# A two-block network on one core: GpSimd makes all four token combinations of the feed-forward layers, in pieces of 512 columns

## The reference, cut to what matters

```python
def swiglu(h, w_in, w_out):
    gu = h @ w_in
    gate, up = jnp.split(gu, 2, axis=-1)
    return (jax.nn.silu(gate) * up) @ w_out
...
for i in range(DEPTH):                # DEPTH = 2
    ...                               # attention, x = x + g1 * y
    h = rmsnorm(x, norm_ffn[i]) * (1 + sc2) + sh2
    x = x + g2 * swiglu(h, ffn_w_in[i], ffn_w_out[i])
```

## Time and profile before

| | us |
|---|---|
| median of 3 runs | 2672.32 |
| lowest, highest | 2672.22, 2672.35 |
| the profiled execution, its own time | 2670.46 |
| span of the profiled execution, first to last instruction | 2668.7 |

### The profile page before, as it was taken

How to read it: one execution, slowest core, us unless ns; L and a number is a source line. 1 busy time by engine, 2 the same in 40 slices (tenths; PEclk the granted TensorE clock), 3 DMA queues, 4 the chain that set the end, 5 groups by cost and what they waited for, 6 DMA issues and landing times. The chain is left out here.

```text
span 2668.7 us, 35605 instructions
## 1 busy us (share of the span) xinstructions
PE 2588.7 (97%) x12898; PEld 2063.0 (77%) x12898; DVE 1885.1 (71%) x3089; ACT 1022.1 (38%) x1833; POOL 331.5 (12%) x455
## 2 busy tenths in 40 slices
PE   6999899999999999999999989999999999999998
PEld 5666587788888888777776768888888887888987
DVE  6888857877777777745656788777777777433565
ACT  5444726333333333445445453333333333111243
POOL 2011003000000000201110210000000027971000
PEclk9999999999999999999999999999999999999999
DMA  6333221111111111223232111111111122113122
GB/s 238 116 129 135 92 90 52 56 51 55 54 52 48 55 55 44 105 68 97 94 105 88 48 32 56 51 51 55 51 55 47 55 63 92 48 48 58 32 95 79
DMA packets 170955, 193.10 MB, mean 72 GB/s; under 512 B 8000, under 2 KB 136224, under 8 KB 170432
## 3 DMA queue, kind: packets, MB, share of 16 engines
q1 hardware_dynamic: 158256, 147.45, 17.1%
q0 software_dynamic: 12592, 44.21, 5.4%
HBM read 177.86 MB, written 12.58 MB: 71 GB/s over the span
## 5 line engine op out<-in xcount | busy, mean ns | idle before, releaser
L2534 DVE SCALAR_TENSOR_TENSOR xT<-psum,mod,xT 128x1024 f32<-128x1024 f32 x352 | 446.2, 1279 | 146.1 <-PE psum L1506 146.0
L1506 PE MATMUL psum<-hT_high,w_low 128*128 128x512 f32 x1344 | 360.5, 390 | 6.7 <-DVE xT L2534 6.6
L1506 PEld LDWEIGHTS psum<-hT_high,w_low 128*128 128x128 f32 x1344 | 251.6, 188 | 62.7 <-DVE xT L2534 11.0
L1964 ACT ACTIVATE w_high<-wpair 128x512 fp32r<-128x512 f32 x294 | 184.8, 632 | 244.3 <-DMA wpair<-in_ffn_w_in_dram 132.8
L1192 PE MATMUL psum<-hT_high,w_low 128*128 128x512 f32 x864 | 244.2, 395 | 2.3 <-DVE arena L3047 2.1
L1506 PE MATMUL psum<-h_low,w_low 128*128 128x512 f32 x672 | 207.6, 390 | 2.2 <-DVE h_low L2529 2.2
L1275 PE MATMUL psum<-hT_high,w_low 128*128 128x512 f32 x480 | 202.1, 421 | 0.9 <-DVE h_low_mix L2472 0.7
L1474 PE MATMUL psum<-hT_high,w_high 128*128 128x512 f32 x504 | 196.6, 390 | 0.0
L1475 PE MATMUL psum<-h_low,w_high 128*128 128x512 f32 x504 | 196.6, 390 | 0.0
L1476 PE MATMUL psum<-hT_high,w_low 128*128 128x512 f32 x504 | 196.4, 390 | 0.0
L1192 PEld LDWEIGHTS psum<-hT_high,w_low 128*128 128x128 f32 x864 | 162.6, 190 | 39.1 <-issue 2.5
(11 more groups left out here) (380 smaller groups left out, 5156.0 us busy)
## 6 DMA issues: line engine op xcount, KB each, us to landing
wpair<-in_ffn_w_in_dram SPq DMA_DIRECT2D x176, 256.0 KB, 2.9
wpair<-in_ffn_w_out_dram SPq DMA_DIRECT2D x88, 256.0 KB, 2.7
wpair<-in_ada_tiles_dram POOLq DMA_DIRECT2D x20, 1024.0 KB, 5.3
wpair<-in_ada_tiles_dram POOLq DMA_DIRECT2D x32, 512.0 KB, 3.6
wpair<-in_w_in_dram SPq DMA_DIRECT2D x24, 512.0 KB, 3.8
wpair<-in_b_tiles_dram SPq DMA_DIRECT2D x18, 512.0 KB, 3.3
arena<-in_ada_tiles_dram SPq DMA_DIRECT2D x8, 1024.0 KB, 16.3
out_dram<-xT SPq DMA_DIRECT2D x16, 512.0 KB, 3.3
```

The lines of the kernel that those rows point to most:

```text
L1506: mm = nc.tensor.matmul(dst[:, HALF * t:HALF * t + HALF], w, src[:, t, :], start=n == 0, stop=n == 2)
L1964: nc.scalar.activation(part_high[name], part_raw[name], ACT.Copy).then_inc(part_high_ready, 1)
L2534: nc.vector.scalar_tensor_tensor(xT[:, m, :], acc[m % 2] if src is None else src, mod[:, l, 40 + m:41 + m], xT[:, m, :], ALU.mult, ALU.add ...
```

## The change

GpSimd makes all four combinations, each in four pieces of 512 columns (16 instructions a layer where there were 6), in the order T1, T3, T2, T4. A piece waits for the pieces that it reads, for the `shift` of the chunk that it reads, and, before it overwrites a raw chunk, for the `half_low` that still reads it. T3 and T4 leave VectorE's list (two instructions of 128 x 2048 a layer). T3's high part takes the place of T1's on ScalarE, and the other way round; T3's low part moves ahead of the first two `add_down` on VectorE. The low parts of T2 and T1 get a second wait, for the combination that still reads the raw values.

```diff
+TOKEN_TURN = ("T1", "T3", "T2", "T4")
+HIGH_TOKENS = ("T3", "T1", "T2", "T4")
...
+def token_number(f, name):
+
+    return 16 * f + 4 * TOKEN_TURN.index(name) + 4
...
                     pool.wait_ge(shifted, shift_number(2 * f + 1, k))
                     nc.gpsimd.tensor_tensor(h_low[:, k, 0:HALF], token_raw[quadrant[0][k // 4]][:, k % 4, :], as_f32(hT_high[:, k, 0:HALF]),
                                             ALU.subtract).then_inc(front_ready, 1)
-                for k in range(4):
-                    pool.wait_ge(shifted, shift_number(2 * f + 1, k, 1))
-                    nc.gpsimd.tensor_tensor(token_raw["T1"][:, k, :], token_raw["T3"][:, k, :], token_raw["B11"][:, k, :],
-                                            ALU.subtract).then_inc(token_made, 1)
-                for n in range(2):
-                    rows = slice(2 * n, 2 * n + 2)
-                    pool.wait_ge(token_made, 8 * f + n + 5)
-                    nc.gpsimd.tensor_tensor(token_raw["T2"][:, rows, :], token_raw["T2"][:, rows, :], token_raw["T1"][:, rows, :],
-                                            ALU.subtract).then_inc(token_made, 1)
+                for n, (name, x, y, read, shift) in enumerate((("T1", "T3", "B11", None, 0), ("T3", "T2", "T3", 0, 4),
+                                                               ("T2", "T2", "T1", 4, None), ("T4", "T4", "T2", None, None))):
+                    for k in range(4):
+                        if n:
+                            pool.wait_ge(token_made, 16 * f + 4 * n + k - 3)
+                        if shift is not None:
+                            pool.wait_ge(shifted, shift_number(2 * f + 1, shift + k, 1))
+                        if read is not None:
+                            pool.wait_ge(h_ready, h_number(2 * f + 1, read + k))
+                        nc.gpsimd.tensor_tensor(token_raw[name][:, k, :], token_raw[x][:, k, :], token_raw[y][:, k, :],
+                                                ALU.subtract).then_inc(token_made, 1)
...
-                def token(n, name):
-
-                    act.wait_ge(token_made, 8 * f + n + 4)
+                def token(name):
+
+                    act.wait_ge(token_made, token_number(f, name))
                     nc.scalar.activation(token_high[name], token_raw[name], ACT.Copy).then_inc(token_high_ready, 1)
...
-                    token(1, "T3")
+                    token("T1")
                     keep(1, "P3", gate_half[:, 1, :], bank["c"])
                     high(1, "S1")
-                    token(3, "T2")
+                    token("T2")
...
-                    token(4, "T4")
+                    token("T4")
...
                 hidden_high(0, 0, first=True)
-                token(0, "T1")
+                token("T3")
                 second_step()
...
-                def token(n, name, x, y, ks):
-
-                    dve.wait_ge(token_made, 8 * f + n + 4)
-                    nc.vector.tensor_tensor(token_raw[name][:, ks], token_raw[x][:, ks], token_raw[y][:, ks], ALU.subtract).then_inc(token_made, 1)
-
-                def token_lows(n, name):
-
-                    dve.wait_ge(token_high_ready, 4 * f + n + 1)
+                def token_lows(name, after):
+
+                    dve.wait_ge(token_high_ready, 4 * f + HIGH_TOKENS.index(name) + 1)
+                    if after:
+                        dve.wait_ge(token_made, token_number(f, after))
                     nc.vector.tensor_tensor(token_low[name], token_raw[name], as_f32(token_high[name]), ALU.subtract).then_inc(token_split, 1)
...
-                    token(0, "T3", "T2", "T3", slice(0, 4))
+                    token_lows("T3", None)
                     add_down(0, 0)
                     add_down(0, 1)
-                    token_lows(1, "T3")
                     add_down(0, 2)
                     down_lows(0, 1)
                     low(1, "S2")
                     combine(1, "S1", first=True)
-                    token(3, "T4", "T4", "T2", slice(0, 4))
-                    token_lows(2, "T2")
+                    token_lows("T2", "T4")
                     dve.wait_ge(product_kept, kept_number(f, 1, "P1"))
                     add(1, "X0", gate_half[:, 0, :], gate_half[:, 0, :], bank["b"], "P2")
                     low(1, "S1")
-                    token_lows(0, "T1")
+                    token_lows("T1", "T2")
                     add_down(0, 3)
                     low(1, "A22")
-                    token_lows(3, "T4")
+                    token_lows("T4", None)
```

## The result

The changed kernel takes 2682.62 us (median of five runs, 2679.87 to 2683.89) against 2672.22 (five runs): ratio 1.0041 [1.0028, 1.0055], slower by 0.4%. The profiled execution took 2681.51 us, span 2679.7; before 2670.46 and 2668.7.

A forecast was written before the change was run, and what follows sets the result against it. PE, 97% busy, was taken as the bound, with VectorE's list setting the pace before the loop. Two layers at +5.3 us give 10.6 on 2670.46, so 2681.1; the median stands 1.86 above: 2683 us, range 2674 to 2689.

The forecast's parts named there:

- Turns on the list that feeds P1 to P3: From 433 us, VectorE's two-SBUF instructions alternate with GpSimd's pieces; the list ends 8.8 us late at S4's low part.
- side sum: Estimate from GpSimd's port rate, 0.85 us a piece for the measured 1.15: total +1 us in place of +10.6.
- The second rival: VectorE keeps the port pair in close runs: stalls 4.3 us for 8.8, +0.9 a layer, 2674.1 us; chance 0.13.
- S3's low part: On VectorE after the PSUM-input pair: shares out T4's other pieces with the next two low parts, itself ending at 450.97.
- PE's waits: New PE idle: 2.0 us before P1, 2.4 before P2, 1.6 and 1.3 around the first `down`.
- T4's removal gives nothing: Between S1 and T2's low part, VectorE waits for ScalarE's high parts anyway, so the 4.8 us there stays.
- Nothing else costs: ScalarE's swap of T1 and T3 and the second waits of T2's and T1's low parts cost nothing; no DMA moved.
- The clock: Rival: more PE gaps lower its granted clock, one or two more falls a layer, 2686 to 2690 us; chance 0.09.
- the stalls: Lateness at S1, 5.25 us a layer: 8.8 lost, 3.0 gained, 0.5 less waiting for PE; 10.6 over two layers.

The follow-up runs named there:

- the 2048-column run: Changed kernel with T3, T2 and T4 each made by one GpSimd instruction of 2048 columns instead of four of 512: 2691.81 us, ratio 1.0068.
- The last run: Changed kernel with VectorE's list reordered, including X0 ahead of S4's low part and T3's low part behind the first `add_down`: 2671.10 us, ratio 0.9994.
- the order alone: Kernel before, nothing moved to GpSimd, four moves in VectorE's list (S1, X0, T3's low part earlier; A11's low part with sixth `add_down` behind X1): 2662.11 us.
- the 16-column run: Changed kernel with its twelve new pieces a layer (T3, T2, T4) cut from 512 columns to 16, waits and orders kept: 2665.72 us, ratio 0.9978.

## Why the prediction was right

The time was forecast at 2683 us, and 2682.62 was measured. The steps, one by one:

- **Turns on the list that feeds P1 to P3: right.** Moved by the 1.00 us of the start, A11's low part was forecast to end at 443.89 and ended at 443.83, A12's low part at 449.01 and 448.90. The Trainium skill, "SBUF — State Buffer", section "Who interferes with whom", says that the second to issue blocks until the first ends; the trace agrees (S3 at 1.77, 1.22 and 0.71 us as the pieces shrink). The prediction's side sum with its estimate of 0.85 us a piece is off: the same list worked through with 0.85 has S4's low part at 451.2 and S1 some 1.5 us late, an estimate of about +3 us, not +1. The forecast did not use it. The second rival, VectorE keeping the pair, fell with these rows and with the 2048-column run.
- **S3's low part: mis-sized.** It was forecast to share out T4's pieces, ending at 451.97 with the shift; it started at 450.01, after the PSUM pair, took 0.68 and was not stalled. S4's low part so ended at 454.62 in place of 455.91. POOL's last piece, 427.90 + 27.87 = 455.77, stalled T3's low part instead (3.38 us in place of 2.28). It ended at 457.92, close to the forecast 458.1. The first `add_down` behind it lets PE's next `down` start, and the third `add_down` waits for that one (460.87, 0.50 us idle), so the earlier P3 gained less than S4's low part did: S1 ended at 463.96 in place of 464.7, 4.51 us late a layer where 5.25 was forecast. By the trace POOL's next piece started at 450.00, 0.01 us ahead of S3's low part, and yet came second: a near tie. The last run has the same list up to there and shows the other outcome: there POOL's piece started at 449.16, S3's low part at 449.18, and it took 1.81 us, as forecast.
- **PE's waits: right in place, somewhat long.** 2.0 us before P1 and 2.4 before P2 were forecast, 1.72 and 2.01 measured; of the 1.6 and 1.3 around the first `down` only the 0.95 before P3 came, since the low parts of the hidden block and of S4 ended earlier.
- **T4's removal gives nothing: right.** VectorE waits 2.50 us for ACT between S1 and T2's low part; with T4 alone moved the time rises, and with S1 moved ahead (the order alone) the wait is gone.
- **Nothing else costs: borne out** as a whole by the 16-column run, which has every other edit and is faster.
- **The clock: a rival that came in part.** The granted clock is 0.91 in the mean of 456 to 476 us where it was 1.00, after PE's new idle stretches, and 0.86 in the second layer's stretch from 1586 us where it was 0.93: more time at 1.2 GHz. The fall in the first of these stretches cost nothing. It lies in P6, and the `down` behind P6 waits for an `add_down` as before: it starts at 473.40, which less 1.00 is 4.50 after 467.90, as late as T2's low part. A second fall cost, in the matmuls from 490.19. They stand behind the same wait as in the first layer of before, where the clock held, and in the second layer of before, where it fell. PE's timeline, after, then the two layers of before:

```profile
473.40 1.20 PE L1515 MATMUL psum<-hT_high,w_low 128*128 128x512 f32 x4
...
490.19 1.22 PE L1515 MATMUL psum<-h_low,w_low 128*128 128x512 f32 x2 [1.13 <-DVE h_low L2535]
```

```profile
482.37 1.20 PE L1506 MATMUL psum<-hT_high,w_low 128*128 128x512 f32 x4 [1.92 <-DVE xT L2534]
484.69 0.73 PE L1506 MATMUL psum<-h_low,w_low 128*128 128x512 f32 x2 [1.12 <-DVE h_low L2529]
...
1594.95 1.22 PE L1506 MATMUL psum<-h_low,w_low 128*128 128x512 f32 x2 [1.13 <-DVE h_low L2529]
```

The last `add_down` of the next step is 5.47 us late in the first layer and 5.05 in the second: 1.0 and 0.5 more than T2's low part was. This goes to the clock, as nothing else on that stretch had changed; that the change brought the falls is not shown. The row of 482.37 also corrects the prediction: its 1.92 us belong among PE's largest waits, ahead of the 1.38 and the 1.54.

Twice 4.5 us of stalls and 1.5 of clock make 10.5, and the medians differ by 10.4. So the total came out nearer than its terms: the stalls were forecast at 10.6, and the clock, at nothing, made up what they lacked. Part of that is luck. The spans of the two traces differ by 11.0, and besides these terms by 1.0 at the first layer's start, by 2.2 the other way between the layers, and by 1.7 around 2213 us, at the end of the second layer, where the clock fell in the trace after (0.83 in the mean of 2210 to 2220 us) and not in that of before (1.00 from 2201 to 2211). The first two were not followed up.

## What to carry to other kernels

A subtraction moved to GpSimd is not free while VectorE runs a dense list with two SBUF inputs: each turn costs VectorE about the length of a piece. Shorter pieces cost less (256 columns still lost 4.4 us here). The pair that reads PSUM kept its pace beside the pieces, so that is a place to put them, which no run here tried. Before an instruction is taken off an in-order list, ask what the next one waits for: T4's 2.28 us were under a wait for ACT. When the bound is the order of one engine's list, change the order first: four moves in VectorE's list gained 10 us, where moving work to another engine lost 10.

## What had not been expected of the hardware

A 512-column subtraction on GpSimd with the same input twice and another output type held VectorE for less (S3 at 1.52 us for 1.77); which of the two did it is not shown. Similar waits of PE dropped the granted clock in one run, or one layer, and not in another: with 3.45 us idle before P6 the first layer of before stayed at 1.00, and after, with no wait above 2.6, it did not. The exception of the earlier trace rows, a 16-column piece that waited through three VectorE instructions, has no explanation here; the 16-column pieces of the first experiment showed nothing like it.
